# Head and attention steps moved to other slots and banks, and the new mLSTM state made by four full-height matmuls in place of eight of 32 rows

## The reference

```
z   = rms_norm(x) @ w_in                    -> attention q, k, v; mLSTM q, k, v, gates, output gate
att = differential attention (4 heads, two softmaxes each), per stream and for the prompt
hm  = mlstm_chunkwise(...)                  # 4 heads
      num   = A @ v + iw * (C q);   den = ...;   h = num / den
      C_new = dec * C + einsum('bhs,bshe,bshd->bhed', sw, v, k)     # per stream b: 16 rows s
x   = x + concat(att, hm) @ w_out
y   = x + square(relu(rms_norm(x) @ w_up)) @ w_down                 # 2048 -> 8192 -> 2048
```

## Time and profile before

| what | value |
|---|---|
| time, median of 3 runs | 1858.93 us (1858.41 to 1859.51) |
| time of the profiled execution | 1858.41 us |
| its span, first to last instruction | 1856.6 us |
| TensorE busy | 1818.2 us, 98% |
| VectorE busy | 892.7 us, 48% |
| ScalarE busy | 696.4 us, 38% |
| mean granted TensorE clock | 0.996 |
| chain that ended last | TensorE 93%, VectorE 2%, ScalarE 2% |

### The profile page before, as it was taken

How to read it: one execution, slowest core, us unless ns; L and a number is a source line. 1 busy time by engine, 2 the same in 40 slices (tenths; PEclk the granted TensorE clock), 3 DMA queues, 4 the chain that set the end, 5 groups by cost and what they waited for, 6 DMA issues and landing times.

```text
span 1856.6 us, 29129 instructions
## 1 busy us (share of the span) xinstructions
PE 1818.2 (98%) x9893; PEld 1661.9 (90%) x9893; DVE 892.7 (48%) x1726; ACT 696.4 (38%) x1335; POOL 151.7 (8%) x195
## 2 busy tenths in 40 slices
PE   6999998999999999999999999999999999999998
PEld 4999987999989999999988999888999888999886
DVE  3443575455556666645434454443445433454433
ACT  4222553544445444433323333322333333333322
POOL 2020000000021101111000011000011000011000
PEclk9999999999999999999999999999999999999999
DMA  8374434656476644344333444333444333444442
GB/s 222 94 221 115 112 96 130 193 181 197 107 207 179 197 132 125 102 124 124 125 125 124 125 124 124 124 126 126 124 125 124 128 127 124 125 124 124 141 141 90
DMA packets 325705, 254.42 MB, mean 137 GB/s; under 512 B 11488, under 2 KB 283152, under 8 KB 325648
## 3 DMA queue, kind: packets, MB, share of 16 engines
q1 hardware_dynamic: 308928, 214.46, 39.3%
q0 software_dynamic: 11072, 37.56, 6.2%
q10 hardware_dynamic: 5648, 1.65, 0.4%
HBM read 234.79 MB, written 18.84 MB: 137 GB/s over the span
## 4 chain that ended last, share of the span: by engine, by line
PE 93%; DVE 2%; ACT 2%; issue 1%; SPq 1%; DMA 0%; DVEq 0%; POOL 0%; ACTq 0%; POOLq 0%
PE acc L485 19%; PE acc L486 19%; PE acc L487 19%; PE bank L508 8%; PE bank L509 8%; PE bank L507 8%; PE bank L1652 4%; PE bank L1659 2%; PE ssb L507 2%; PE ssb L508 2%; PE ssb L509 2%; PE ssb L1652 1%; ACT w_hi L451 1%; SPq L435 1%; PE bank L1811 0%
## 5 line engine op out<-in xcount | busy, mean ns | idle before, releaser
L460 DVE TENSOR_TENSOR w_lo<-raw,w_hi 128x512 fp32r<-128x512 f32 x768 | 556.0, 730 | 840.5 <-ACT w_hi L451 838.3
L451 ACT ACTIVATE w_hi<-raw 128x512 fp32r<-128x512 f32 x768 | 483.4, 630 | 865.8 <-PE acc L487 504.6
L485 PE MATMUL acc<-a_hi,w_hi 128*128 128x400 f32 (+1 forms) x1024 | 365.7, 357 | 0.0
L486 PE MATMUL acc<-a_lo,w_hi 128*128 128x400 f32 (+1 forms) x1024 | 354.2, 346 | 0.0
L487 PE MATMUL acc<-a_hi,w_lo 128*128 128x400 f32 (+1 forms) x1024 | 353.6, 345 | 0.0
L486 PE MATMUL acc<-x2g_lo,w_hi 128*128 128x384 f32 x1024 | 348.0, 340 | 0.0
L485 PE MATMUL acc<-x2g_hi,w_hi 128*128 128x384 f32 x1024 | 345.7, 338 | 0.9 <-DVE y_rows L1601 0.9
L487 PE MATMUL acc<-x2g_hi,w_lo 128*128 128x384 f32 x1024 | 344.6, 337 | 0.0
L508 PE MATMUL bank<-w_lo,a_hi 128*128 128x512 f32 x640 | 252.9, 395 | 0.0
L509 PE MATMUL bank<-w_hi,a_lo 128*128 128x512 f32 x640 | 252.5, 395 | 0.0
L507 PE MATMUL bank<-w_hi,a_hi 128*128 128x512 f32 x640 | 251.9, 394 | 0.0
(11 more groups left out here) (290 smaller groups left out, 1247.6 us busy)
## 6 DMA issues: line engine op xcount, KB each, us to landing
raw<-in_w_up SPq DMA_DIRECT2D x128, 512.0 KB, 4.0
raw<-in_w_down SPq DMA_DIRECT2D x128, 512.0 KB, 3.5
raw<-in_w_in SPq DMA_DIRECT2D x96, 512.0 KB, 4.0
raw<-in_w_out SPq DMA_DIRECT2D x32, 512.0 KB, 4.0
kc<-in_cache_k POOLq DMA_DIRECT2D x8, 1024.0 KB, 7.0
vc<-in_cache_v POOLq DMA_DIRECT2D x8, 1024.0 KB, 8.7
C_rows<-in_state_C POOLq DMA_DIRECT2D x8, 512.0 KB, 6.0
out<-C_rows POOLq DMA_DIRECT2D x8, 512.0 KB, 4.9
```

The lines of the kernel that those rows point to most:

```text
L451: e.activation(w_hi[:, q], raw[:, slot, 4 * (q % 2):4 * (q % 2) + 4, :], ACT.Copy).then_inc(hi_ready, 1)
L460: e.tensor_tensor(w_lo[:, q], raw[:, slot, 4 * (q % 2):4 * (q % 2) + 4, :], w_hi[:, q].bitcast(F32), ALU.subtract).then_inc(lo_ready, 1)
L485: e.matmul(out, w_hi[:, q, kk], hi[:, k, at], start=start, stop=False, skip_group_check=True)
L486: e.matmul(out, w_hi[:, q, kk], lo[:, k, at], start=False, stop=False, skip_group_check=True)
```

## The change

The attention starts one slot later (`FIRST_PAIR` 5), and its `oturn` goes from bank 1 to bank 4. The heads start at slot 0 and are 14 slots apart. In a head, `ksw` moves from slot 1 to slot 7 (behind `og`), `states` and `weigh` one slot later, `cp` from 7 to 11, `hturn` and `gate` from 11 to 12, `mix` from 12 to 13. `cn` is cut into four steps at slots 8 to 11, each with its own matmul and its own take in the same slot. That matmul contracts over all 128 rows and writes four streams (512 columns) of one half of the state, in banks 1, 2, 1, 2; `cp` uses bank 0 and the numerators 3, 4, 0. The number of instructions that VectorE needs to take the states is the same.

```
-FIRST_PAIR, PER_PAIR, TILE_LATER = 4, 8, 4
+FIRST_PAIR, PER_PAIR, TILE_LATER = 5, 8, 4
-HEAD_AT = (("rows", 0), ("decay", 0), ("scores", 1), ("expo", 1), ("ksw", 1), ("states", 2), ("weigh", 3), ("cn", 4),
-           ("take0", 4), ("take1", 5), ("take2", 5), ("take3", 6), ("num", 6), ("hsum", 6), ("cp", 7), ("og", 7),
-           ("hroot", 8), ("hturn", 11), ("gate", 11))
+HEAD_AT = (("rows", 0), ("decay", 0), ("scores", 1), ("expo", 1), ("states", 3), ("weigh", 4), ("num", 6), ("hsum", 6),
+           ("og", 7), ("ksw", 7), ("hroot", 8), ("cn0", 8), ("cn1", 9), ("cn2", 10), ("cn3", 11), ("cp", 11),
+           ("hturn", 12), ("gate", 12))
-PER_HEAD = 13
-FIRST_HEAD = 2
+PER_HEAD = 14
+FIRST_HEAD = 0
...
-        plan.append((max(s + 12, last + 5 + h), "mix", h))
-    plan.append((FIRST_HEAD + PER_HEAD * (NH - 1) + 10, "nout", 0))
+        plan.append((max(s + 13, last + 5 + h), "mix", h))
+    plan.append((FIRST_HEAD + PER_HEAD * NH - 1, "nout", 0))
...
-            u.add(("oT", STEPS[n]), 1)
+            u.add(("oT", STEPS[n]), 4)
...
-                u.add(("num", x, h), (4, 0, 1)[x])
+                u.add(("num", x, h), (3, 4, 0)[x])
...
-            for i in range(4):
-                u.add(("cn", h, i), i)
+            u.add(("cn", *h), (1, 2, 1, 2)[h[1]])
         elif what == "cp":
-            u.add(("cp", h), 2)
+            u.add(("cp", h), 0)
...
             def new_state(h, i):
                 b = take(e, ("cn", h, i))
-                for half in range(2):
-                    for x in range(2):
-                        s_, at = 2 * i + x, (2 * half + x) * P
-                        ins = stt(C_rows[:, s_, half], C_rows[:, s_, half],
-                                  iwB[:, h, TD * s_ + TD - 1:TD * s_ + TD], b[:, at:at + P], ALU.mult, ALU.add)
+                half, b0 = i // 2, 4 * (i % 2)
+                for s_ in range(b0, b0 + 4):
+                    ins = stt(C_rows[:, s_, half], C_rows[:, s_, half],
+                              iwB[:, h, TD * s_ + TD - 1:TD * s_ + TD], b[:, (s_ - b0) * P:(s_ - b0 + 1) * P],
+                              ALU.mult, ALU.add)
                 taken(ins, ("cn", h, i))
...
-            def new_state(h):
+            def new_state(h, i):
                 e.wait_ge(S("k_sw_made"), h + 1)
-                banks = [fill(e, ("cn", h, i)) for i in range(4)]
-                for half in range(2):
-                    for i in range(4):
-                        rows = slice(32 * i, 32 * i + 32)
-                        last = mm(banks[i][:, 2 * half * P:2 * (half + 1) * P], v_rows[rows, 0, half * P:(half + 1) * P],
-                                  k_sw[rows, 2 * i:2 * i + 2].rearrange("p s d -> p (s d)"), True, True)
-                        if half:
-                            filled(last, ("cn", h, i))
+                b = fill(e, ("cn", h, i))
+                half, b0 = i // 2, 4 * (i % 2)
+                filled(mm(b[:], v_rows[:, 0, half * P:(half + 1) * P],
+                          k_sw[:, b0:b0 + 4].rearrange("p s d -> p (s d)"), True, True), ("cn", h, i))
```

More of the change, by code:

```diff
@@ L153, in head_plan @@
         for what, at in HEAD_AT:
-            plan.append((s + at, "take", (h, int(what[4:]))) if what.startswith("take") else (s + at, what, h))
-        plan.append((max(s + 12, last + 5 + h), "mix", h))
-    plan.append((FIRST_HEAD + PER_HEAD * (NH - 1) + 10, "nout", 0))
+            plan.append((s + at, "cn", (h, int(what[2:]))) if what in ("cn0", "cn1", "cn2", "cn3") else (s + at, what, h))
+        plan.append((max(s + 13, last + 5 + h), "mix", h))
+    plan.append((FIRST_HEAD + PER_HEAD * NH - 1, "nout", 0))
     return in_order(plan)
@@ L970, in head_work @@
                     yield slot
-                    vo = None if what == "take" else mvo[:, h % 2]
+                    vo = None if what == "cn" else mvo[:, h % 2]
                     if what == "rows":
@@ L1551, in head_work @@
                         state_keys(h)
-                    elif what == "take":
+                    elif what == "cn":
                         new_state(*h)
@@ L1896, in head_work @@
                     elif what == "cn":
-                        new_state(h)
+                        new_state(*h)
                     elif what == "cp":
```

## The result

| kernel | median us | lowest to highest | profiled execution: time, span, mean clock |
|---|---|---|---|
| before | 1859.22 (4 runs) | 1858.41 to 1861.42 | 1858.41, 1856.6, 0.996 |
| changed | 1916.97 (4 runs) | 1912.87 to 1919.51 | 1921.78, 1920.0, 0.989 |

The ratio of the changed kernel to the one before is 1.032, with a 95% interval of 1.0304 to 1.0336: slower. 1912 us was forecast, with a range of 1887 to 1932. The median is that of four executions. All 21 on record run from 1912.87 us (mean clock 0.992) to 1922.34 (0.987), with a median of 1919.78.

A forecast was written before the change was run, and what follows sets the result against it. The prediction took TensorE's queue as the path, with the other engines' side work hidden under it. Its terms, 18 - 2 + 4.4 + 8.6 + 18.5 + 0 + 1 + 5 = +53.5 us on 1858.4, gave 1912 us, range 1887 to 1932.

The forecast's parts named there:

- Bank 4: Attention, 15 slots: TensorE's turned weights wait 1.2 us each for ScalarE to read `oturn` from bank 4, +18 us.
- Start of the attention: Attention one slot later: the 2.5 us wait goes, most of the 2.0 stays, about 1 us may come; -2 us.
- Entry: First head step: TensorE comes 4.4 us early and waits for the loads, +4.4 us.
- `cn` on TensorE: Heads: four full-height matmuls of 0.86 us in place of eight banded ones taking 1.28 us, +8.6 us in all.
- `ksw`: Heads: `cn0` waits for `ksw` behind `og` in slot 7, 4.2 us in three heads, 5.9 in head 1; +18.5 us.
- Clock: TensorE's clock falls behind five new waits longer than 4 us, 1.5 us each, less up to 3 at `cp`; +5 us.
- (a): Rival: the bank 4 wait in the attention is hidden, 1894 us; chance 0.12.
- (b): Rival: in the heads `cn0` finds `ksw` ready; the wait and its part of the clock go, 1889 us; chance 0.12.
- (c): Rival: both (a) and (b); matmuls, entry and end stay, 1871 us; chance 0.08.
- (d): Rival: the clock falls at every wait, the 15 of 1.2 us in the attention too: +22, 1934 us; chance 0.10.
- (f): Rival: nothing reaches TensorE's queue, gains and costs cancel, 1855 to 1862 us; chance 0.03.
- (e): Rival: later first pair removes 4.5 us at the attention's start, no new waits or matmul cost; 1854 us; chance 0.03.

The follow-up runs named there:

- e5: The kernel before with `oturn` in bank 4 in place of bank 1 and nothing else: 1877.27 us.
- e1: The changed kernel with `oturn` back in bank 1: 1903.15 us.
- e2: The changed kernel with `ksw` back in slot 1: 1894.67 us.
- e3: The changed kernel with `ksw` ahead of `og` in slot 7: 1896.56 us.
- e6: The kernel before with `cn` as four full-height matmuls of 512 columns in slot 4, in banks 0 to 3: 1867.47 us.
- e8: The kernel before with VectorE's mask of the bias moved from slot 0 to slot 3, behind the value copies: 1856.19 us.
- e10: e8 with each value transposition waiting only for its own tile, and the first keys in slot 1 in place of 0: 1850.92 us.
- e4: The changed kernel with the heads starting at slot 2 and 13 slots apart: 1918.06 us.
- e7: The changed kernel with `oturn` in bank 1, `ksw` in slot 1, and heads from slot 2, 13 slots apart: 1872.79 us.
- e9: e8 with the first `ko` in slot 3 in place of 2: 1856.48 us.
- e11: e9 and e10 together, on the kernel before: 1852.05 us.

## Why the prediction was right

- **What bounds the kernel.** Right. Idle time and busy time of TensorE add up to the whole change, 39.5 + 23.9 = 63.4 us, while VectorE was busy for 1.4 us more and ScalarE for 2.3 us.
- **Bank 4.** +18 forecast; 16.9 us of waits in the changed kernel, and e5 alone gave +18.2. What the step missed, that in the later phase bank 1 would cost 4.0 us itself, was found only in e1.
- **Start of the attention.** -2 forecast, -1.8 measured: the value and key waits went from 4.8 (2.5, 2.0 and 0.3) to 3.0. The new wait of about 1 us in the slot of the last value copies is there with 1.3.
- **Entry.** +4.4 forecast, 4.4 measured, which is in part luck. In e1, e2 and e3 the slots between the last output and the first head step are the same, and the wait was 2.9, 2.5 and 2.6 us: the last load took 6.7, 6.2 and 6.4 us to land, where it took 8.2 in the changed kernel's profile. The mechanism is right, and its price lies between 2.5 and 4.4, as the prediction's own remark on the loads allows.
- **`cn` on TensorE.** +8.6 forecast; e6 gave 8.4 in the time and 9.2 in the timeline (4 x 2.3). The matmul's price of 0.86 us, scaled from one of 400 columns, is what `cn1` shows: 1.04 us to the second matmul, less one step of 0.18.
- **`ksw`.** +18.5 forecast, 17.5 measured; the longest, 5.7 us, for 5.9. That it is the chain and not the load was shown by e3.
- **Next head's states and end.** 0 and +1 forecast; 0.9 in one head, and 0.8.
- **Clock: the term that was mis-sized.** The step said five long waits would cost 1.5 us each and took +5 in all. That they would cool the clock was right, and that the 15 short ones would not. But 1.5 was read at the slots of `cp`. Behind the five long waits the half speed cost 12.4 us in the profiled execution, 2.5 each on average. Nor were the 3 us for falls at `cp` saved, since it still fell in two heads, as before. The term is about +12 there and not +5, an estimate from the windows of 1 us; e3, which has no such wait, is 14.4 us less busy. The median of four is 4.8 us under this execution, and part of that can be falls, whose number differs.
- **The sum.** 53.5 forecast; 58 in the medians of four, 63.4 in the profiled execution. The clock makes 7 us of the gap on the profiled one, 1.3 are scatter at the launch, and 2.6 are the busy time that isn't taken apart; the other terms together came out 1 us under the forecast.

Of the rivals, (a) is refuted by e5, (b) by the profile and e3, and (c) with them; (d) by the clock of 1.00 over the attention's slots, and (f) by the time. Rival (e) had a true kernel: the start of the attention did hold something to win (e8, e10), but the first pair's slot was not the way to it.

## What to carry to other kernels

Where one engine's queue is the path and others are fed from it, price a plan by who stands ahead in the reader's own queue: a bank claimed twice in one slot costs the reader's whole queue ahead of it (its split and its reads, 1.2 us), each time. Put a step that the bounding engine will ask for ahead of steps which wait for a third engine; e3 won 20 us by exchanging two names. A long wait of TensorE can be dearer than it looks, here 3.9 us idle and 2.5 us at half clock behind it. Where one has to be paid, the runs speak for several short ones: in five profiles with 15 short waits each, the clock fell behind one of the 75.

## What the runs showed of the hardware

The granted clock fell to 0.50, the 1.2 GHz level, behind all 13 of the waits of 3.9 to 5.7 us in the heads and at the entry (the changed kernel, e1, e4). Behind shorter waits it goes both ways, and the length alone doesn't decide:

- Of the 75 waits at the turned weights (the changed kernel, e2, e3, e4, e5; 1.1 to 1.8 us), one was followed by a fall, that of 1.6 us which ends at 360.9 us in e2. The same wait, 1.6 us too, was not in e3 and e4.
- At the first head step it fell behind 1.6 us in e4, and not behind 2.9, 2.5, 2.6 and 2.3 in e1, e2, e3 and e7.
- One wait of 2.2 us that ends at about 70 us, the same in every kernel, was followed by a fall in e3, e5 and e7 and by none in the other ten.
- The wait of 2.6 us for `m` where the attention starts was followed by a fall in each kernel that had it, up to e9; the one of 2.6 for `av_rows` in e11 was not.
- The waits for `ksw` in e3, up to 2.9 us, were not; the one of 2.5 at `cn2` in e2 was.

The windows of e2 around the first of these:

```profile
356.00:360.00 4.00, 3.17 (x19) 2.59 (x17) 1.19 (x5) 2.09 (x6) 1.40 (x2) 1.00 0.48 113
360.00:364.00 4.00, 3.13 (x13) 3.11 (x14) 1.71 (x4) 1.25 (x5) 0.00 (x0) 0.72 0.99 403
```

And in the kernel before it fell twice with TensorE never idle, in the slots of `cp`, whose matmuls have 128, 8 and 1 columns. e10, whose heads are the same, shows 0.91, 1.00 and 0.88 over the three such stretches of 14 us, e9 1.00, 1.00 and 0.88. Which of the heads are hit changes from one kernel's profile to the next, by 1.7 us for each fall (windows of 1 us). A chain of small matmuls can so cost clock as a wait does.
